# Two RMS norms done by halves of the tokens, a new order at the opening, and two steps moved in the retention, in a single-core two-block transformer kernel

## The reference

```python
# block 1
h = rmsnorm(x, attn_pre_g)
proj = h @ w_in                          # q, k, v, gates of 8 sparse and 8 sliding-window heads
mix = concat(o_nsa, o_swa) @ w_o
x = x + rmsnorm(mix, attn_post_g)        # called y1 in the kernel: mix; x1: the new x
h = rmsnorm(x, mlp_pre_g)
a, u = split(h @ w_gate_up)
y = (gelu(causal_dwconv(a)) * u) @ w_down
x = x + rmsnorm(y, mlp_post_g)           # y2: y; x2: the new x
x = x + (p @ w_ple) * sigmoid(x @ w_ple_gate)
# block 2
h = rms_norm(x, norm_mix)                # neighbourhood attention and retention from h @ w_in_2
x = x + concat(na_out, ret_out) @ w_out_2
x = x + square(relu(rms_norm(x, norm_mlp) @ w_up_2)) @ w_down_2
return rms_norm(x, norm_final)
```

## Time and profile before

| | |
|---|---|
| time, median of 3 runs | 1300.33 us (1300.19 to 1302.67) |
| the profiled execution: its own time | 1301.79 us |
| its span | 1300.0 us (1.8 us lie around it) |
| TensorE busy | 1277.9 us, 98% |
| VectorE busy | 801.6 us, 62% |
| ScalarE busy | 634.8 us, 49% |
| GpSimd busy | 155.2 us, 12% |
| TensorE on the chain that ended last | 88% (VectorE 7%, ScalarE 2%) |

### The profile page before, as it was taken

How to read it: one execution, slowest core, us unless ns; L and a number is a source line. 1 busy time by engine, 2 the same in 40 slices (tenths; PEclk the granted TensorE clock), 3 DMA queues, 4 the chain that set the end, 5 groups by cost and what they waited for, 6 DMA issues and landing times.

```text
span 1300.0 us, 16626 instructions
## 1 busy us (share of the span) xinstructions
PE 1277.9 (98%) x6104; PEld 1062.6 (82%) x6104; DVE 801.6 (62%) x1553; ACT 634.8 (49%) x1239; POOL 155.2 (12%) x146
## 2 busy tenths in 40 slices
PE   7999999999999999999999999999999999999998
PEld 7888888868888888888778777888888888888887
DVE  5789799685654556345788786578644333344335
ACT  6687576454334443233455655476543242342344
POOL 0021120000010001000002101022311020020111
PEclk9999999999999999999999999999999999999999
DMA  7211110422332333332332211432323323233321
GB/s 267 90 42 41 42 41 18 157 76 90 100 96 73 114 105 94 97 94 81 113 90 83 91 61 57 127 105 77 97 91 96 98 81 113 82 106 89 105 89 65
DMA packets 64623, 118.19 MB, mean 91 GB/s; under 512 B 7712, under 2 KB 12192, under 8 KB 64288
## 3 DMA queue, kind: packets, MB, share of 16 engines
q1 hardware_dynamic: 62848, 112.95, 28.3%
q10 hardware_dynamic: 1696, 4.19, 1.0%
HBM read 115.02 MB, written 2.10 MB: 90 GB/s over the span
## 4 chain that ended last, share of the span: by engine, by line
PE 88%; DVE 7%; ACT 2%; issue 2%; DMA 1%; POOL 0%; SPq 0%; POOLq 0%; DVEq 0%; ACTq 0%
PE bank L581 26%; PE bank L583 26%; PE bank L582 25%; PE bank L781 2%; PE bank L662 2%; PE bank L664 2%; PE bank L663 2%; DVE pp L2105 1%; PE bank L767 1%; PE bank L768 1%; DVE ptl L2128 1%; DVE pp L2122 1%; PE bank L735 1%; DMA praw<-in_pT 0%; DVE qs L2021 0%
## 5 line engine op out<-in xcount | busy, mean ns | idle before, releaser
L1934 DVE TENSOR_TENSOR wl<-raw,wh 128x512 fp32r<-128x512 f32 (+2 forms) x360 | 265.8, 749 | 329.6 <-ACT wh L1268 328.9
L1268 ACT ACTIVATE wh<-raw 128x512 fp32r<-128x512 f32 (+1 forms) x398 | 242.3, 619 | 288.8 <-PE bank L583 276.0
L581 PE MATMUL bank<-AH,wh 128*128 128x512 f32 (+1 forms) x848 | 333.7, 393 | 1.0 <-DVE AL L1948 0.3
L583 PE MATMUL bank<-AH,wl 128*128 128x512 f32 (+1 forms) x848 | 328.8, 388 | 0.0
L582 PE MATMUL bank<-AL,wh 128*128 128x512 f32 (+1 forms) x848 | 327.0, 386 | 0.0
L581 PE MATMUL bank<-BH,wh 128*128 128x512 f32 x624 | 247.9, 397 | 1.4 <-DVE wl L1934 1.4
L583 PE MATMUL bank<-BH,wl 128*128 128x512 f32 x624 | 244.6, 392 | 0.0
L582 PE MATMUL bank<-BL,wh 128*128 128x512 f32 x624 | 243.1, 390 | 0.0
L583 PEld LDWEIGHTS bank<-AH,wl 128*128 128x128 f32 x848 | 159.3, 188 | 35.6
L581 PEld LDWEIGHTS bank<-AH,wh 128*128 128x128 f32 x848 | 159.8, 188 | 34.8 <-issue 4.1
L582 PEld LDWEIGHTS bank<-AL,wh 128*128 128x128 f32 x848 | 159.5, 188 | 32.7 <-issue 0.2
(11 more groups left out here) (319 smaller groups left out, 1627.8 us busy)
## 6 DMA issues: line engine op xcount, KB each, us to landing
raw<-in_w_dn SPq DMA_DIRECT2D x104, 256.0 KB, 2.6
raw<-in_w_gu SPq DMA_DIRECT2D x88, 256.0 KB, 2.6
raw<-in_w_up SPq DMA_DIRECT2D x64, 256.0 KB, 2.6
raw<-in_w_nsa SPq DMA_DIRECT2D x16, 256.0 KB, 2.7
raw<-in_w_pg SPq DMA_DIRECT2D x16, 256.0 KB, 2.6
raw<-in_w_naq SPq DMA_DIRECT2D x16, 256.0 KB, 2.7
nbi<-in_na_bias ACTq DMA_DIRECT2D x8, 448.0 KB, 3.4
raw<-in_w_swa SPq DMA_DIRECT2D x10, 256.0 KB, 2.8
```

What stands on the lines that cost most here:

```text
L581: t.matmul(o, w, xh, start=start, stop=False, skip_group_check=skip)
L583: return t.matmul(o, wl, xh, start=False, stop=stop, skip_group_check=skip)
L1268: a.activation(W[i % NW].h[:, 0:n], RAW[i % NRAW][:, 0:n], ACT.Copy).then_inc(*s_wh.up(i))
L1934: v.tensor_tensor(w.l[:, 0:n], RAW[i % NRAW][:, 0:n], w.h[:, 0:n], ALU.subtract).then_inc(*s_wl.up(i))
```

## The change

It has four parts. **Opening**: the transfer of the constants is issued by ScalarE's queue and no longer by SyncE's, ahead of everything else there; TensorE runs 8 products of `ones` by `ones` (fp32, 128x128) that nobody reads; chunk 0 of the first product is taken as 4 high by high products when the two high parts are there, 4 with the chunk's low part, and 4 with the piece's low part. **Norms y1 and y2**: the table for the root is loaded behind the seventh square; the eighth chunk is added, squared and summed in two halves of 256 tokens. **First chunk of x1 and x2**: scaled, added and split by halves, and TensorE's first high products run by halves (16 of 256 columns in place of 8 of 512). In y1 the weight pieces that stood ahead of these steps on ScalarE and VectorE now stand behind them. **Retention**: on VectorE the low parts of two pieces (`w_ret` 7 and `w_mid` 0) come before `rotated_low(0)` and `rotated(1)`. The core of the diff (the same edits for `y2`/`x2` as for `y1`/`x1` are cut):

```diff
 def product(...):  # fresh
-                        e.wait_ge(s_xh.at((fresh, ks[0])))
-                        for g in range(G):
-                            b, free = bs[g]
-                            e.wait_ge(*free)
-                            t.matmul(b[:, :], w.h[:, g * P:g * P + P], x.h, start=True, stop=False)
-                        for g in range(G):
-                            t.matmul(bs[g][0][:, :], w.l[:, g * P:g * P + P], x.h, start=False, stop=False)
+                        for h in range(2):
+                            o = of_tokens(h)
+                            e.wait_ge(s_xh.at((fresh, ks[0], h)))
+                            for g in range(G):
+                                b, free = bs[g]
+                                e.wait_ge(*free)
+                                t.matmul(b[:, o], w.h[:, g * P:g * P + P], x.h[:, o], start=h == 0, stop=False, skip_group_check=True)
+                                t.matmul(b[:, o], w.l[:, g * P:g * P + P], x.h[:, o], start=False, stop=False, skip_group_check=True)
...
-            def tokens(name, src, ready, N, mids):
+            def tokens(name, src, ready, N, mids, warm=0):
...
+                for n in range(warm):
+                    t.matmul(bs[3][:, 0:P], ones[:, :], ones[:, :], start=True, stop=True)
                 for k in range(8):
...
+                    if warm and k == 0:
+                        i = WHERE[name, 0]
+                        w = W[i % NW]
+                        e.wait_ge(s_xh.at(("x0", 0)), s_wh.at(i))
+                        for b in range(4):
+                            t.matmul(bs[b][:, 0:N], x.h[:, P * b:P * b + P], w.h[:, 0:N], start=True, stop=False)
+                        e.wait_ge(ready(0))
+                        for b in range(4):
+                            t.matmul(bs[b][:, 0:N], x.l[:, P * b:P * b + P], w.h[:, 0:N], start=False, stop=False)
+                        e.wait_ge(low(i))
+                        for b in range(4):
+                            m = t.matmul(bs[b][:, 0:N], x.h[:, P * b:P * b + P], w.l[:, 0:N], start=False, stop=False)
+                        m.then_inc(*s_mm.up(("p", i)))
+                        continue
...
             def squares_of(key, src, first, last, *done, halves=False):
                 for i in range(4):
+                    if halves and i % 2 == 0:
+                        e.wait_ge(s_sq.at((key, 7, i // 2)))
...
-            tokens("w_vtok1", A, x0, 408, {})
+            tokens("w_vtok1", A, x0, 408, {}, warm=8)
...
 def scalar(e):
+            def squares_by_halves(key, x, done):
+                for h in range(2):
+                    e.wait_ge(s_sv.at((*done, h)), *sqr.before((key, 7)))
+                    a.activation(sqr.ap((key, 7))[:, of_tokens(h)], x[:, of_tokens(h)], ACT.Square).then_inc(*s_sq.up((key, 7, h)))
+                sqr.read((key, 7), (s_st, (key, "c", 7)))
...
+            a.dma_start(cst[:, 0:c_used[0]], ins["consts"]).then_inc(*s_c.up("in", by=16))
             e.wait_ge(s_z.at("ones"))
...
             for c in range(8):
+                if c == 7:
+                    root_table("y1")
+                    break
                 hi(WHERE["w_o_nsa", c] + 4)
...
-                if c == 7:
-                    root_table("y1")
                 out1(c)
+            squares_by_halves("y1", chunk(ACC, 7), ("y1", 7))
+            hi(WHERE["w_o_nsa", 7] + 4)
             soon("y1")
...
                     for j, (name, k, _) in enumerate(DOWN3):
                         hi(WHERE[name, k] + 4)
                         ff_last(c0 + n - 2, j, c0, free)
+                        if j == 6:
+                            root_table("y2")
...
-            root_table("y2")
-            down_out(2, 7)
-
+            squares_by_halves("y2", chunk(ACC, 7), ("dn", 2, 7))
...
 def vector(e):
+            def x1_first(h):
+                o, t, b = of_tokens(h), tmp.ap(("x1", 0)), bank.ap(("bk", "y1"))
+                e.wait_ge(s_st.at(("bk", "y1")), *tmp.before(("x1", 0)))
+                v.scalar_tensor_tensor(out=t[:, o], in0=chunk(ACC, 0)[:, o], scalar=g_post[:, 0:1], in1=b[:, o], ...)
+                e.wait_ge(s_dv.at(("x1", 0, h)), s_x2[0].at("in"))
+                v.tensor_tensor(chunk(X, 0)[:, o], chunk(X, 0)[:, o], t[:, o], ALU.add).then_inc(*s_sv.up(("x1", 0, h)))
+
+            x1_first(0)
+            x1_first(1)
             behind("w_ple", 0)
-            x1_scaled(0)
-            x1_sum(0)
             x1_scaled(1)
...
             rotated(0)
+            behind("w_ret", 3)
+            ahead("w_ret", 4, 2)
             rotated_low(0)
             rotated(1)
-            behind("w_ret", 3)
-            ahead("w_ret", 4, 2)
             straight(2)
...
 def sync(e):
-            d.dma_start(cst[:, 0:c_used[0]], ins["consts"]).then_inc(*s_c.up("in", by=16))
```

92 lines of the change are left out of this document (68 added, 24 removed).

## The result

The changed kernel takes 1297.29 us in the median of 7 runs (1295.45 to 1297.68), the kernel before 1300.21 in the median of 7 (1298.73 to 1302.67). The ratio is 0.9968, with a 95% interval of 0.9959 to 0.9978: 0.32% or 2.9 us less. Five more runs of the changed kernel, in a later set, gave 1295.94 and a ratio of 0.9969 (0.9956 to 0.9981). Over all 12 its median is 1297.0, and over all 70 runs of the kernel before 1300.7. The 12 runs lie in two groups, five at 1295.2 to 1295.9 and seven at 1296.9 to 1297.9, so their median says which group is the larger one; their mean is 1296.6.

What follows compares the result with a forecast made beforehand. TensorE, 98% busy, was taken as the bound, so only its idle time and slow clock could be won. 3.0 + 2.1 + 0.25 + 0.5 = 5.85 us from 1301.79 gave 1295.9; adjusted for the median, 1295.3, range 1293.3 to 1298.2.

Steps and rivals of the forecast that it cites:

- its own sign: Opening: the prediction called itself wrong if TensorE's sum of squares ended after 24 us; it expected about 22.9.
- The transfer of chunk 0 is issued at 0.74 in place of 1.18: Opening: with the constants off SyncE's queue, ScalarE's and VectorE's work on chunk 0 comes 0.44 us sooner.
- the other 84 products take 15.2: Opening: after chunk 0's 12 products, TensorE's remaining ones take 15.2 us at full clock and end at 22.9.
- 1.4 or 3.3 by when it rises: Opening: bounds of the gain, 1.4 us if the clock rises 4.2 us after the first real product, 3.3 at best.
- Rival (1): Opening: unread products don't raise the clock in time, or the gap behind loses it; gain 1.4 us, 1296.9; chance 0.13.
- The idle 0.66: y1: TensorE's wait for the eighth square, until 263.22, would go, since the half square ends by 262.4.
- The idle 0.70 ahead of 261.48 stays: y1: TensorE's wait ahead of the first squares remains, 0.70 us, since it waits for the seventh square's sum.
- without the fall in before y1 gives 1.0: y1: against runs of the old kernel without the slow-clock stretch, the gain is 1.0 us and not 2.1.
- The load's price: y1: the root's table load delays the next square by 1.40 us, by the trace; the skill page gave 2.66.
- The wait for chunk 1's low part: y2: TensorE waits 1.0 us less for x2's first chunk, then waits for the second's low part; net 0.25 us.
- The new wait of about 0.9: Retention: a wait ahead of the value product replaces the removed 1.41 us one, so only 0.5 us is kept.
- Rival (5): Attention: the shifted program meets further slow-clock stretches, 1.7 us each, four more needed to cross 1300.3; chance 0.03.

Runs made afterwards that it cites:

- the partial runs: Two runs: changed kernel with the eighth weight rounded ahead of y1's table load, 1297.77 us; changed kernel with old norms, unread products filling y1's waits, 1298.01 us.

## Why the prediction was right, and where it was off

The forecast was 1295.3; it came to 1297.29, and 1297.0 over 12 runs. The direction and the places were right, the mechanisms of y1, y2 and the retention too, and that of the opening in part; the range held it. The sum was 5.85 against the profiled execution, where the two profiles differ by 4.64. That so close a sum came of them is partly luck: the falls near 110 and 772, which no edit is shown to bring or take, moved it by +0.9 and -1.6. By its own sign the opening would have been wrong with a sum after 24. It was 23.98 here, and 25.3 to 26.0 in the four profiles with eight unread products and a late rise.

**Opening: 3.0 predicted, 2.1 found.** The step that failed is "The transfer of chunk 0 is issued at 0.74 in place of 1.18 [...] Everything that ScalarE and VectorE do for chunk 0 hangs on it: 0.44 us." The first activation came 0.08 sooner (4.40 against the 4.48 of before), since it hangs on the constants too, and these landed 3.6 us after their issue and not 1.9. They were now issued at the same moment as the first chunk of the input, and from ScalarE's queue; which of the two delays them was not tested. I had costed their issue and not their landing. The first real product so came at 5.70 and not at 5.25. A second term was too small as well, "the other 84 products take 15.2": they took 15.93 (8.05 to 23.98). Here 0.08 per chunk is the wider spacing, 2.24 us for 12 products and not 2.16, and some 0.2 was lost in the first two of these chunks. The clock's rise was bounded rightly in kind (1.4 or 3.3 by when it rises) but not in size: with a late rise the eight-product openings stood 0.1 to 0.8 us ahead of before and not 1.4. The opening of before was itself a matter of the run, 26.11 in one profile and 27.47 in another. Over the profiles, the mean sum of the eight with eight unread products is 24.7 and of the two old openings 26.8, which gives 2.1, and the run that undid the opening cost 2.2.

The sentence on the section on the clock gate of the Trainium skill's page "TensorE: Matmul & The Clock Gate", that the rise varies from run to run, was confirmed by the table above: 3.86 to 12.73 us. Rival (1), that the unread products don't raise the clock in time, happened in half of the profiles with eight. It was given 0.13, and rather than excluding the forecast it mixes with it.

**y1: 2.1 predicted, 2.75 and 2.81 found.** The idle 0.66 went, the clock stayed up, and the halves cost what was said: from the first scaling at 263.82 to the weight's low part at 265.53 is 1.71, against 1.64. The term that was mis-sized is "The idle 0.70 ahead of 261.48 stays": it was 0.24 in this profile and 0.17 in the next, for the reason told above, the landing ahead of it, and no edit did that. Without that part y1 gave 2.3, near the 2.1. The prediction said that without the fall in before y1 gives 1.0; the partial runs give 0.25 + 0.5 = 0.75 for that, and 1.5 for the clock, where 1.1 was said. The load's price was the trace's and not the page's: here the half square started 1.40 behind the load's start, as in the earlier trace rows, against the 2.66 worked out from the page "ScalarE: Activation LUTs" of the Trainium skill.

**y2: 0.25 predicted, 0.15 found.** The wait for chunk 1's low part took the place of the one for the first chunk, as said, with 0.67 us.

**Retention: 0.5 predicted, 0.28 found in both profiles, of which 0.26 is the edit's.** The new wait of about 0.9 ahead of the value product was there with 1.06. This is the place where a wait of 1.4 us bought 0.3, because the low scores were next: ScalarE's copies for them start at 741.32, straight behind one of its swaps (L1736). That this chain does not hang on TensorE is read from the timeline and was not tested.

**The rest.** The remaining distance is no part of the change: a stretch at half rate near 772 in the changed kernel's profile (1.6 us lost) and one near 110 in that of before (0.9 us won). Rival (5) had named this mechanism, further slow stretches elsewhere, at 1.7 us each and with four needed; near 772 there was one in 2 of the 13 profiles with one-column products. The parts undone one by one cost 2.2 + 2.6 + 0.35 = 5.2 us, against a difference of 3.7 between the medians of the two kernels. A part of the surplus lies outside the program: 7 of the 22 runs with the opening or the norms undone spent 2.1 to 2.8 us outside their span, where the two kernels always spent 1.8 or 1.9. By the spans the costs are 1.85 + 2.25 + 0.25 = 4.35, against 3.75. The remaining 0.6 is open; the opening's and y1's costs are largely those of the clock, and these come in some runs and not in others.

## What to carry to other kernels

Let unread products reach up to the first real one: with some idle microsecond between them the early rise of the clock was a toss (4 of 8), and with ten or eleven that left none it came in 3 of 3, which is likely and not proven. When a transfer is moved to another queue, ask what its landing releases and not only what its issue costs. In a tight norm the load of a function's table belongs directly behind the last operation that needs none, and waits of 0.5 to 0.7 us on each side of small products cost more by the clock (1.5 us) than by themselves (0.75 us).

## What was not expected of the hardware

TensorE's granted clock fell to half near 772 us in 2 of 13 profiles, in work in which TensorE was busy without a break. The same instructions ran at full rate in the other 11. The rise at the start varied from 3.86 to 10.59 us with the same instructions ahead of it. The spacing of the first matrix's products at full rate was 0.180 us in 3 profiles and 0.187 in 11, with no edit to tell them apart. And the five unread products in y1's waits removed the fall there at no cost that can be seen: the second squares started at 259.85, where the filling's records end (258.95 + 0.89), and 0.06 behind the end of the square that they need (259.79), against 0.05 with the norms undone.
